# The opening of a two-block transformer kernel: modulation rows in shift and scale pairs, two projection chunks in slices

## The reference, cut to what matters

```python
mod = jax.nn.silu(c) @ ada_w[i] + ada_b[i]                     # 6 x 1024 values
sh_a, sc_a, g_a, sh_f, sc_f, g_f = jnp.split(mod[:, None, :], 6, axis=-1)
h = rms_norm(x, attn_norm[i]) * (1.0 + sc_a) + sh_a
# sparse_mixer:
mq, mk, mv, nq, nkv, ng = jnp.split(h @ w_in, SPARSE_SPLITS, axis=-1)
#   columns of w_in: mq 0:512, mk 512:1024, mv 1024:1536, nq 1536:2048, nkv 2048:2816, ng 2816:2840
#   q and k heads: rms_norm over 64 values, then a rotary turn of the first 16
```

## Time and profile before

| | us |
|---|---|
| median of 3 runs | 2206.93 |
| lowest and highest | 2206.03, 2209.4 |
| the profiled execution | 2206.92 |
| its span | 2205.1 |
| PE busy in the span | 2156.8 (98%) |
| DVE busy | 1847.5 (84%) |
| ACT busy | 1327.8 (60%) |
| POOL busy | 112.2 (5%) |

### The profile page before, as it was taken

The page is one execution under the profiler, slowest core; times in us unless marked ns, Lnnn a source line. Parts: engine busy times, 40 slices in busy tenths (PEclk is TensorE's granted clock), DMA queues, the critical chain, the costliest instruction groups (busy, mean ns, idle before and its releaser), DMA issues.

```text
span 2205.1 us, 31747 instructions
## 1 busy us (share of the span) xinstructions
PE 2156.8 (98%) x12960; PEld 1899.6 (86%) x12960; DVE 1847.5 (84%) x2321; ACT 1327.8 (60%) x1495; POOL 112.2 (5%) x155
## 2 busy tenths in 40 slices
PE   6999999999999999999999999999999999999998
PEld 4888999889999879999798888888888888888886
DVE  7966888876998677888896989989897988989896
ACT  3574443665333776434633777777776777777775
POOL 3000111000010000010000000000000000000021
PEclk9999999999999999999999999999999999999999
DMA  9855988625787616885652899989998999989992
GB/s 369 299 190 201 340 331 303 229 77 217 299 310 263 224 39 253 310 327 185 217 189 117 339 371 365 370 337 360 373 360 337 368 366 369 370 337 357 374 360 85
DMA packets 137361, 633.30 MB, mean 287 GB/s; under 512 B 9305, under 2 KB 21626, under 8 KB 115195
## 3 DMA queue, kind: packets, MB, share of 16 engines
q1 hardware_dynamic: 112698, 536.83, 64.9%
q0 software_dynamic: 24512, 94.38, 11.4%
HBM read 630.13 MB, written 1.05 MB: 286 GB/s over the span
## 4 chain that ended last, share of the span: by engine, by line
PE 82%; DVE 11%; DMA 3%; issue 2%; ACT 1%; SPq 0%; DVEq 0%; ACTq 0%
PE ps L1266 80%; DVE wring_rounded L3211 3%; DMA aring<-in_ada_rows 3%; DVE aring L3238 2%; DVE work L3211 1%; PE ps L2391 1%; DVE OT L3235 1%; PE ps L1469 1%; DVE F L3218 1%; DVE F L3211 0%; PE ps L1444 0%; DVE work L3750 0%; ACT aring_rounded L2472 0%; ACT scr_rounded L2472 0%; ACT F_rounded L2472 0%
## 5 line engine op out<-in xcount | busy, mean ns | idle before, releaser
L3211 DVE TENSOR_TENSOR wring_rounded<-wring,scr_rounded 128x2048 fp32r<-128x2048 f32 (+1 forms) x314 | 569.4, 1844 | 58.2 <-ACT scr_rounded L2472 57.8
L2472 ACT ACTIVATE scr_rounded<-wring 128x2048 fp32r<-128x2048 f32 (+1 forms) x314 | 479.7, 1553 | 181.3 <-PE ps L1266 123.9
L1266 PE MATMUL ps<-wring_rounded,OT_rounded 128*128 128x512 f32 (+1 forms) x1184 | 314.8, 390 | 2.7 <-DVE wring_rounded L3211 1.8
L1266 PEld LDWEIGHTS ps<-wring_rounded,OT_rounded 128*128 128x128 f32 x1184 | 220.1, 188 | 47.4 <-DVE wring_rounded L3211 2.4
L3238 DVE CUSTOM_DVE_ANT_0 aring<-aring,F,vec 128x1024 f32<-128x1024 f32 x152 | 187.9, 1282 | 34.0 <-DMA aring<-in_ada_rows 33.2
L3211 DVE TENSOR_TENSOR wring_rounded<-wring,H_rounded 128x2048 fp32r<-128x2048 f32 (+1 forms) x85 | 193.8, 2280 | 24.2 <-ACT H_rounded L2472 24.1
L3211 DVE TENSOR_TENSOR wring_rounded<-wring,aring_rounded 128x2048 fp32r<-128x2048 f32 x84 | 193.3, 2302 | 12.4 <-ACT aring_rounded L2472 12.1
L2472 ACT ACTIVATE H_rounded<-wring 128x2048 fp32r<-128x2048 f32 (+1 forms) x85 | 162.4, 1910 | 54.7 <-issue 38.4
L2472 ACT ACTIVATE aring_rounded<-wring 128x2048 fp32r<-128x2048 f32 x84 | 161.2, 1919 | 54.4 <-PE ps L1266 54.4
L1266 PE MATMUL ps<-V_rounded,wring_rounded 128*128 128x256 f32 x1184 | 177.7, 284 | 3.6 <-DVE wring_rounded L3211 3.5
L1266 PE MATMUL ps<-work_rounded,F_rounded 128*128 128x256 f32 x1056 | 169.8, 283 | 0.0
(11 more groups left out here) (391 smaller groups left out, 3698.0 us busy)
## 6 DMA issues: line engine op xcount, KB each, us to landing
wring<-in_moe_gate SPq DMA_DIRECT2D x56, 2048.0 KB, 8.8
wring<-in_moe_up SPq DMA_DIRECT2D x56, 2048.0 KB, 8.9
wring<-in_moe_down SPq DMA_DIRECT2D x56, 2048.0 KB, 8.7
aring<-in_ada_rows POOLq DMA_DIRECT2D x88, 1024.0 KB, 7.5
wring<-in_ffn_w_gate SPq DMA_DIRECT2D x10, 2048.0 KB, 10.8
wring<-in_ffn_w_up SPq DMA_DIRECT2D x10, 2048.0 KB, 14.7
wring<-in_ffn_w_down SPq DMA_DIRECT2D x10, 2048.0 KB, 10.4
wring<-in_diff_w_in SPq DMA_DIRECT2D x6, 2048.0 KB, 15.8
```

The source lines that it names most:

```text
L1266: return pe.matmul(dst, lhsT, rhs, start=start, stop=stop, **kw)
L2472: return act.activation(dst, src, ACT.Copy, **kw)
L3211: return ve.tensor_tensor(dst, x, y, op)
```

## The change

- **Loads.** The eight transfers now hold one tile of shift rows and the same tile of scale rows each (128 + 128 rows), so that tile k of the input can be finished after transfer k. `con`, positions, rotary gains, `vec` and `X` go first. Behind transfer k - 1 stand two slices of 128 features x 512 columns (256 KB each), of the chunks 2048:2560 and 1536:2048. The order of the chunks after that is 2560:2840, 0:512, 512:1024.
- **POOL** now makes H = X x root for each tile (`by_root`), ahead of the rotary tables; ACT first copies the spread root from PSUM into `rstd`.
- **ACT** loads the table of the root ahead of the squares; per tile it writes upper and full modulated input (two instructions of 256 columns) and the two upper slices; the sines with their two table loads come after tile 0.
- **DVE** per tile: two modulation instructions, `gsc` of the tile, then the rest of the input tile before and the rests of its two slices. `inverse(0)` stands behind the first pair. The small work on angles and lambda stands ahead of all.
- **PE** per tile: 6 idle products, then 12 products (2 chunks x 2 token blocks x 3 passes); then the 280-column chunk, the transposes of the nq rows, the chunk 0:512, and from there as before.
- **ACT and DVE after the tiles** run in another order: the parts 4 and 5 are now those of the 280-column chunk, and the two q or k chunks that are already multiplied are worked off between the parts 4 to 7.

The core of the diff:

```diff
@@ loads (SP)
-            load_first(0)
-            sp.dma_start(vec[:], a["vec"]).then_inc(vec_loaded, 16)
             sp.dma_start(con[:, 0:FIRST_CON], a["con"][:, 0:FIRST_CON]).then_inc(vec_loaded, 16)
-            load_first(1)
...
+            sp.dma_start(vec[:], a["vec"]).then_inc(vec_loaded, 16)
             sp.dma_start(X[:], a["x"]).then_inc(x_loaded, 16)
...
+            load_first(0)
+            for k in range(1, KT):
+                load_slices(k - 1, ada0_loaded[k])
+                load_first(k)
+            load_slices(KT - 1, last_slice_loaded)
...
-            for j, lo, n in ((1, 2560, 280), (2, 1536, 512), (3, 0, 512), (4, 512, 512)):
+            for j, lo, n in ((2, 2560, 280), (3, 0, 512), (4, 512, 512)):
@@ POOL
+            norm_spread[0].emptied(pool)
+            for k in range(KT):
+                pool.tensor_tensor(H[:, k, :], X[:, k, :], rstd[:], ALU.mult).then_inc(by_root, 1)
@@ PE
-            pe.wait_ge(ada_used, 7)
-            idle_products(3, 14)
-            by_token_split(sp_w[0], 0, sp_tok[0], CH, OTupper, Hlower, HI_TILES[0])
+            idle_products(3, 12)
...
+                idle_products(3, 6)
+                pe.wait_ge(hi_tile, k + 1)
+                pe.wait_ge(slice_upper, 2 * k + 2)
+                run(OTupper, False, False)
+                pe.wait_ge(slice_lower, 2 * k + 2)
+                run(OTupper, True, False)
+                pe.wait_ge(lo_tile, k + 1)
+                ins = run(Hlower, False, True)
...
+            for k in range(KT):
+                slice_products(k)
+            pe.sem_inc(part_used, 4)
             pe.wait_ge(con_loaded, 16)
-            by_token_split(sp_w[1], 2, sp_tok[1], 280, OTupper, Hlower)
-            by_token_split(sp_w[2], 4, sp_tok[2], CH, OTupper, Hlower, None, lambda: turn_rows(sp_turn[1], 2))
+            by_token_split(sp_w[2], 4, sp_tok[2], 280, OTupper, Hlower)
+            turn_rows(sp_turn[1], 0)
@@ ACT
+            act.activation(warm[:], C("ones")[:, 0:1], ACT.Sqrt)
             squares(0)
...
+            def shifted_tile(k):
+                act.wait_ge(scaled, k + 1)
+                act.wait_ge(by_root, k + 1)
+                scale, shift = gsc[:, k:k + 1], mod[:, 0, k:k + 1]
+                affine(OTupper[:, k, :], H[:, k, :], scale, shift).then_inc(hi_tile, 1)
+                affine(H[:, k, :], H[:, k, :], scale, shift).then_inc(x_shifted, 1)
+            def round_slices(k):
+                slice_loaded(act, k)
+                if k >= 2:
+                    act.wait_ge(slice_used, k - 1)
+                for j in range(2):
+                    copy(slice_part(j, k), slice_weights(j, k, False)).then_inc(slice_upper, 1)
+            for k in range(KT):
+                shifted_tile(k)
+                round_slices(k)
+                if k == 0:
+                    rotary_angles()
@@ DVE
+            add_first(0)
+            scale_tile(0)
             inverse(0)
-            for n in range(5, 8):
-                add_first(n)
-            ve.wait_ge(ada_used, 8)
-            scale_of(0, 8, vec[:, VEC["attn_norm"][0]:VEC["attn_norm"][0] + 8])
-            root = inverse_rows(0)
-            for k in range(KT):
-                stt(H[:, k, :], X[:, k, :], gsc[:, k:k + 1], root, ALU.mult, ALU.mult).then_inc(scaled, 1)
...
+            for k in range(1, KT):
+                add_first(k)
+                scale_tile(k)
+                lower_tile(k - 1)
+                for j in range(2):
+                    slice_rest(j, k - 1)
+            lower_tile(KT - 1)
+            for j in range(2):
+                slice_rest(j, KT - 1)
             ve.wait_ge(rotary_made, 4)
             ve.wait_ge(con_loaded, 16)
+            part_rest(sp_w[2], 4, 280)
+            row_sums(0, 8)
+            part_rest(sp_w[2], 5, 280)
+            rows(0, sp_tok[1], 8, ((0, 0, 8, 4),), None)
...
+            row_sums(2, 8)
+            part_rest(sp_w[3], 6)
+            rows(2, sp_tok[0], 8, ((0, 0, 2, 5), (4, 4, 2, 6)), sp_turn[1])
+            part_rest(sp_w[3], 7)
+            row_sums(4, 2)
+            rows(4, sp_tok[2], 2, ((0, 6, 2, 7),), None)
             add_more(0)
...
+            part_rest(sp_w[4], 8)
             add_more(1)
```

More of the change, by code:

```diff
@@ L520, in build @@
         sp_hi = Chunk(ring, dmas=0)
-        sp_w = [Chunk(ring) for _ in range(5)]
+        sp_w = [Chunk(ring, dmas=0 if j < 2 else 1) for j in range(5)]
         sp_hi_end = Chunk(ring, dmas=0)
@@ L524, in build @@
         sp_w.append(Chunk(ring))
-        sp_tok = [[J(2 * (j % 2) + qt) for qt in range(2)] for j in range(6)]
+        sp_tok = [[J(b + qt) for qt in range(2)] for b in (0, 4, 2, 6, 0, 2)]
         sp_turn = [None] + [[J(4), J(5)] for _ in range(4)]
@@ L2667, in _ @@
-            act.activation(work[:, 1568:1584], work[:, 1440:1456], ACT.Sin, scale=-1.0).then_inc(rotary_made, 1)
-            act.activation(warm[:], C("ones")[:, 0:1], ACT.Sqrt)
-            deviation(0)
-            round_part(sp_w[0], 0)
-            shifted(0, mod[:, 0, 0:8], OTupper)
-            for n in range(1, 3):
-                round_part(sp_w[n // 2], n, 280 if n == 2 else CH)
+            deviation(0)
+            norm_spread[0].filled(act)
+            copy(rstd[:], PS[norm_spread[0].b][:, 0:T]).then_inc(norm_spread[0].bank.free, 1)
```

150 lines of the change are left out of this document (86 added, 64 removed).

## The result

| | before | changed |
|---|---|---|
| median, us | 2206.91 (4 runs) | 2232.76 (4 runs) |
| lowest, highest | 2206.03, 2209.4 | 2221.56, 2240.32 |
| profiled execution, its span | 2206.92, 2205.1 | 2221.56, 2219.8 |
| PE busy in the span | 2156.8 | 2174.6 |

The changed kernel is slower by 1.1%: ratio 1.0114, 95% interval [1.0092, 1.0136]. 2212.5 us was forecast with a range of 2202 to 2218; the direction was right and the size was not. Two things are to be explained: 14.64 us in the profiled execution, where 5.6 were expected, and a spread of 19 us between runs of a kernel whose predecessor spreads over 3 (over 4 to 8 in the four later sessions, 62 runs). The profiled execution is the fastest of the four; the median lies 25.85 us above the kernel before.

A forecast was written before the change was run, and what follows sets the result against it. The opening was taken as bound by DVE's chain to about 80 us, then PE. Part 9's delay of +3.9 and the clock's +1.7 made +5.6 on 2206.92: 2212.5 us, range 2202 to 2218.

The forecast's parts named there:

- What bounds the kernel: Opening: a DVE chain up to about 80 us, then PE; they meet at part 9, DVE with 1.5 us in hand.
- Loads and root: Start: X lands at 9.2, first pair at 11.75, root and inverse at 17.6 us, DVE idle 3.0 us ahead of it.
- Tiles 0 and 1 and the port: First tiles: DVE idle 1.4 and 1.1 us; slowing by POOL on the shared port taken as 0, up to 3.0.
- The pitch of tiles 2 to 7: DVE bounds these tiles at 4.3 us each, PE's 18 products take 3.9; last slice rest at 52.0.
- Behind the tiles: DVE idle 3.1 and 1.6 us, chunk 3's sums at 85.7; part 9 starts 3.9 us late.
- The clock: PE's 5.5 us idle ahead of part 9 halves the granted clock for 3.4 us: +1.7 us.
- the short row: Earlier profile's half clock of 3.4 us at 1206 us, beside 6.9 us in the opening; used to size the clock at +1.7.
- The later steps: Behind part 9: steps up to the first feed-forward hang on each other, so the shift at 111 us carries unchanged.
- Rival 3: Worse tiles: POOL's port costs 3.0 and the clock 3.4, in all +10.3, 2217.2 us; chance 0.17.

The follow-up runs named there:

- Experiments 3 and 4: Kernel before with ten repeated sums on DVE ahead of chunk 3's sums: 2238.48 us; the same with 24 idle products in PE's pause: 2211.89 us.
- experiment 6: Kernel of experiment 5 with `inverse(0)` put behind the second pair of modulation rows instead of the first: 2218.06 us, ratio 1.0051.
- experiment 10: Changed kernel with 24 idle products filling the pause ahead of part 9, without the 6 idle products ahead of each tile: 2210.15 us, ratio 1.0022.
- experiment 11: Changed kernel with POOL's products X x root of tiles 3 to 7 held back until DVE has scaled tile 2: 2239.5 us in one run.
- experiment 8: Changed kernel with the compression's 64 products of 30 columns put in one row behind the products of parts 9 and 10: 2227.45 us, ratio 1.0091.
- experiment 5: Changed kernel with part 9 rounded ahead of chunk 3's squares and modulation piece 1 behind the rests of parts 9 and 10: 2216.45 us, ratio 1.0053.

## Why the prediction was right and wrong

By its own steps:

- **What bounds the kernel: right.** DVE's chain to the sums of chunk 3, and part 9 as the place where it meets PE. Experiments 3 and 4 confirm it with nothing but DVE's lateness at that place.
- **Loads and root: right within 0.6 us.** X landed at 9.17 (9.2), the first pair of rows at 11.85 (11.75) and the second, which only experiment 6 shows, at 15.90; the inverse came at 18.18 (17.6), DVE idle 3.64 us ahead of it (3.0). But the wait was not worth its 3 us: experiment 6 filled it and won nothing, since the chain through the root sets tile 0.
- **Tiles 0 and 1 and the port: mis-sized.** I took 0 and kept 3.0 for the range. The slice rests of tile 0 took 2.18 instead of 1.28, two modulation instructions 1.75 each and two `gsc` 0.56 each: 0.9 + 0.9 + 0.8 = 2.6 us. My reason for 0, that tiles 0 and 1 have idle time on DVE, failed: DVE waited 1.21 us in tile 0 (1.4), but in tile 1, where I had 1.1 us of waiting behind ACT's sines, not at all. The last slice rest ended at 53.5 (52.0).
- **The pitch of tiles 2 to 7: right, 4.25 us (4.3); PE's part in it wrong.** I had 18 products at 3.9 us and PE waiting. They take 4.24, PE never waited, and the idle products put it 1.6 us behind DVE, 1.7 us of the landmark (experiment 10).
- **Behind the tiles:** DVE idle 1.98, 1.81 and 1.40 us, for which I had 3.1 and 1.6. Sums of chunk 3 at 87.59 (85.7), PE idle in one piece 5.29 us (5.5), part 9 late by 5.85 us (3.9).
- **The clock: the step that failed.** I saw the fall and its place, and sized it by the short row, "since PE works up to that gap": half clock for 3.4 us, +1.7. Measured: 20.6 us and +8.9 in the profiled execution (filling the pause takes 8.6 of them back), 54.6 us and +24 in the execution of experiment 11 with the same pause. That PE works up to the gap bounded nothing. What it does behind the pause mattered (experiment 8: 6.8 us with long products alone), and that was in the order of instructions: the short products of the compression. Behind both stretches of the earlier trace rows PE had other work than this. The short one also stands behind waits of PE of only 0.53 and 0.95 us among small products (at 1202.37 and 1205.60), so the kernel before already showed a fall without a long gap.
- **The later steps:** I carried the shift unchanged to the end. Up to a landmark in the first feed-forward (309.32 before, 324.67 changed) it grew by 0.6 us, with a wait of PE of 1.66 us there in place of 0.40, and the end gave that back: -0.1 in sum in the profiled execution, but up to +4 in others (experiment 5).

In the profiled execution: 5.85 + 8.91 - 0.12 = 14.64. The predicted +5.6 was 3.9 + 1.7; of the 9.04 us missed, 7.21 are the clock and 1.95 DVE, less the 0.12. For the median, 25.85 us above the kernel before, the clock is larger still: filling the pause takes 17.4 us off it. Rival 3, the one on the right side, had the right parts (port and clock), with 3.4 for the clock. The range of 2202 to 2218 had no case in which the clock stays low for longer than the 6.9 us of the earlier trace rows, and the profile of before shows none.

Left open: what decides whether the clock falls in a pause of 1.4 us, and whether it comes back behind the first block of transposes or only behind the second. The runs show both for the same order of work.

## What to carry to other kernels

Price a new idle piece of PE by what PE does behind it. Here the half clock lasted 6.8 us ahead of long products and 17 to 55 us ahead of long and short ones mixed, each us of it cost about half a us, and even a pause of 1.4 us could bring it. Where a wait of PE can't be removed, a handful of idle products in a free bank in exactly that wait is nearly free (7 were worth 15.8 us here); idle products where PE has no wait delay everything behind them. When a schedule is rebuilt, look for the one edge where two chains meet and ask which instruction on the waiting engine could go first: here one rounding moved ahead of the squares, with one modulation piece moved back, let part 9 begin without a pause.

## What was not expected of the hardware

- After one pause the granted clock stayed at half for 17.0 to 54.6 us while PE's records filled nearly all of the stretch.
- Where the clock had fallen ahead of the mix of products, it came back 2.1 to 3.5 us after the start of a block of eight 128x128 transposes in all five executions: in four of them in the middle of the mix, in the fifth only behind the second block, where the mix ends.
- The same pause (1.43 and 1.45 us) at the same place brought 17.2 us of half clock in one execution and none in another; the ten runs of the kernel with the first spread over 25 us.
- 64 products of 30 columns in a row brought the half clock without any pause ahead of them, and PE spent 23.8 us on them.
- POOL's products of 256 columns and DVE's two-operand instructions held each other up both ways: DVE's took 1.75 instead of 1.28 us, POOL's eight took 9.56 us, 1.2 each, instead of 0.61 each. The Trainium skill (SBUF — State Buffer, "Who interferes with whom") has DVE and GpSimd lock each other out of a shared port, and experiment 11 agrees.
